# Two-layer hybrid block on one core: the feed-forward input is rated and split ahead, and two of three products become one of 512 columns

## The reference

```python
def rms_norm(x, g):
    y = xf * lax.rsqrt(jnp.mean(xf * xf, axis=-1, keepdims=True) + EPS)
    return y * g

def conv_ffn(h, w_up, conv_w, conv_b, w_down):
    u = h @ w_up                       # 256 x 1024 by 1024 x 5632
    u = conv_b + sum(conv_w[j] * causal_shift(u, 2 - j) for j in range(3))
    gate, val = jnp.split(u, 2, axis=-1)
    return (jax.nn.silu(gate) * val) @ w_down      # 2816 x 1024

x = x + conv_ffn(rms_norm(x, norm_ffn_g[l]), ...)
```

## Time and profile before

| | us |
|---|---|
| median of 3 runs | 1101.73 (1101.21 to 1103.01) |
| the profiled execution | 1100.96 |
| its span, first to last instruction | 1099.2 |
| PE busy | 1074.0 (98%) |
| weight loads busy (beside PE) | 1020.2 (93%) |
| DVE busy | 826.3 (75%) |
| ACT busy | 600.2 (55%) |

### The profile page before, as it was taken

The page is one execution under the profiler, slowest core; times in us unless marked ns, Lnnn a source line. Parts: engine busy times, 40 slices in busy tenths (PEclk is TensorE's granted clock), DMA queues, the critical chain, the costliest instruction groups (busy, mean ns, idle before and its releaser), DMA issues.

```text
span 1099.2 us, 26063 instructions
## 1 busy us (share of the span) xinstructions
PE 1074.0 (98%) x10078; PEld 1020.2 (93%) x10078; DVE 826.3 (75%) x1393; ACT 600.2 (55%) x891; POOL 10.5 (1%) x24
## 2 busy tenths in 40 slices
PE   8999999999999999999999999999999999999997
PEld 7998898898999999999999889988999999999996
DVE  6798485685787878887869975738767878888776
ACT  6951312666665655555678313137475666555555
POOL 0000000100000000000000000010000000000000
PEclk9999999999999999999999999999999999999998
DMA  8451322444355565555534413134445456555663
GB/s 292 150 173 60 115 79 78 122 138 147 123 174 172 170 194 185 179 173 189 191 119 154 154 59 113 45 106 133 137 147 177 142 170 194 186 175 174 190 185 105
DMA packets 46272, 164.00 MB, mean 149 GB/s; under 512 B 5904, under 2 KB 6080, under 8 KB 46192
## 3 DMA queue, kind: packets, MB, share of 16 engines
q1 hardware_dynamic: 44784, 160.88, 45.6%
q0 software_dynamic: 688, 0.81, 0.4%
q10 hardware_dynamic: 720, 1.14, 0.3%
HBM read 161.24 MB, written 1.05 MB: 148 GB/s over the span
## 4 chain that ended last, share of the span: by engine, by line
PE 88%; DVE 5%; ACT 4%; issue 2%; DMA 1%; SPq 0%; DVEq 0%; ACTq 0%
PE psum L429 87%; DVE sb_lo L1187 1%; ACT sb_rw L854 1%; DVE sb_rw L1265 1%; ACT sb_hi L854 1%; DVE sb_inv L1399 1%; ACT L854 1%; DMA sb_x<-x_t 1%; ACT sb_inv L854 0%; DVE sb_rw L1269 0%; ACT sb_oh L854 0%; DVE sb_rw L1505 0%; DVE sb_rw L1503 0%; ACT sb_rs L854 0%; DVE sb_ol L1206 0%
## 5 line engine op out<-in xcount | busy, mean ns | idle before, releaser
L854 ACT ACTIVATE sb_hi<-sb_raw 128x1024 fp32r<-128x1024 f32 (+1 forms) x300 | 312.0, 1049 | 262.9 <-PE psum L429 258.9
L429 PE MATMUL psum<-sb_hh,sb_hi 128*128 128x256 f32 x1568 | 450.6, 287 | 4.0 <-DVE sb_hl L1194 3.0
L429 PE MATMUL psum<-sb_hl,sb_hi 128*128 128x256 f32 x1568 | 443.6, 283 | 0.0
L429 PE MATMUL psum<-sb_hh,sb_lo 128*128 128x256 f32 x1568 | 443.4, 283 | 0.0
L1187 DVE TENSOR_TENSOR sb_lo<-sb_raw,sb_hi 128x1024 fp32r<-128x1024 f32 x298 | 361.0, 1221 | 72.5 <-ACT sb_hi L854 70.7
L429 PEld LDWEIGHTS psum<-sb_hh,sb_hi 128*128 128x128 f32 x1568 | 300.6, 192 | 10.7 <-issue 6.9
L429 PEld LDWEIGHTS psum<-sb_hl,sb_hi 128*128 128x128 f32 x1568 | 300.8, 192 | 1.0 <-issue 1.0
L429 PEld LDWEIGHTS psum<-sb_hh,sb_lo 128*128 128x128 f32 x1568 | 300.7, 192 | 0.0
L429 PE MATMUL psum<-sb_oh,sb_hi 128*128 128x256 f32 x672 | 193.1, 287 | 7.1 <-DVE sb_ol L1516 4.7
L429 PE MATMUL psum<-sb_oh,sb_lo 128*128 128x256 f32 x672 | 191.3, 285 | 0.0
L429 PE MATMUL psum<-sb_ol,sb_hi 128*128 128x256 f32 x672 | 191.2, 285 | 0.0
(11 more groups left out here) (165 smaller groups left out, 1002.3 us busy)
## 6 DMA issues: line engine op xcount, KB each, us to landing
sb_raw<-w_stream SPq DMA_DIRECT2D x299, 512.0 KB, 4.0
sb_pm<-mix_par ACTq DMA_DIRECT2D x2, 512.5 KB, 3.8
y_t<-sb_rw SPq DMA_DIRECT2D x4, 256.0 KB, 2.3
sb_cf<-const_f SPq DMA_DIRECT2D x1, 739.0 KB, 9.1
sb_pm<-mix_par SPq DMA_DIRECT2D x1, 512.5 KB, 9.7
sb_raw<-w_stream SPq DMA_DIRECT2D x2, 256.0 KB, 3.7
sb_x<-x_t SPq DMA_DIRECT2D x2, 256.0 KB, 4.8
sb_x<-x_t SPq DMA_DIRECT2D x1, 512.0 KB, 6.2
```

The costliest lines, as they stand in the source:

```text
L429: return pe.matmul(out, lhsT, rhs, start=start, stop=stop, skip_group_check=True)
L854: return act.activation(out, in_, func, scale=scale, bias=bias, **kw)
```

## The change

`hh` and `hl` (x times g) stay for tiles 0 to 5. During the first turn of the loop, which is written out now (tiles 2 to 5), DVE and ACT build a second input: x times g times the rates, in float32 (`XR`), its high half and its low half, which lie side by side in the new tensor `o2` (`RATED`, behind the places of `oh` and `ol`, which are now parts of `o2`). The 16 tiles of the four turns that follow multiply this input. The high weights meet high and low half in one matmul of 512 columns (high half's sum in columns 0 to 255 of the bank, low half's in 256 to 511), and the low weights meet the high half in a second matmul of 256. The two sums are joined on the way out: ACT copies columns 256 to 511 to `UM` (`low_half`), DVE adds columns 0 to 255 (`add_up`), which takes the place of `scale_up`. The rates are no longer multiplied there.

```diff
+        oh, ol = o2[:, 0, :, :], o2[:, 1, :, :]
+        RATED = o2[:, :, BT:, :]
+        XR = unit(4, 2).rearrange("p (k t) -> p k t", t=T)
@@ TensorE, ffn_up
+            out = bank[2 * (u % 2) + which]
             for k in range(KT):
+                if rated:
+                    mm(out, hi[:, s, cols], RATED[:, :, k, :], k == 0, False)
+                    last = mm(out[:, 0:T], lo[:, s, cols], RATED[:, 0, k, :], False, k == KT - 1)
+                else:
+                    last = split_mm(out[:, 0:T], ...)
@@ TensorE, the loop
-                with pe.Fori(0, FTURNS) as i:
+                turn(0, False)
+                pe.wait_ge(rated_l, 2 * l + 2)
+                with pe.Fori(1, FTURNS) as i:
+                    turn(i, True)
@@ ACT
+            def low_half(t, u, which, slab):
+                act.wait_ge(slab_done, slab + 1)
+                k = 2 * (u % 2) + which
+                do(UM[:, k, :], bank[k][:, T:2 * T], ACT.Copy).then_inc(low_out, 1)
@@ ACT, a tile of the loop (rated: turns 1 to 4)
                         for which in range(2):
+                            if rated:
+                                low_half(...)
                             conv(l, t, u, which, ..., True)
                         silu(l, t, u)
                         ahead_in(split, l, i, o + 2)
                         product(l, t, u)
+                        if not rated and u in (1, 2):
+                            four = slice(4 * u - 4, 4 * u)
+                            act.wait_ge(rated_x, 2 * l + u)
+                            do(RATED[:, 0, four, :], XR[:, four, :], ACT.Copy).then_inc(rated_h, 1)
@@ DVE
+            def add_up(l, t, u, which):
+                k = 2 * (u % 2) + which
+                dve.wait_ge(low_out, l * 2 * (FT - FU - 2) + 2 * t + (which + 1 - 2 * (FU + 2)))
+                tt(UM[:, k, :], UM[:, k, :], bank[k][:, 0:T], ALU.add).then_inc(up_scaled, 1)
+            def rate(l, u):
+                four = slice(4 * (u % 2), 4 * (u % 2) + 4)
+                if u < 2:
+                    for t in range(4 * u, 4 * u + 4):
+                        ins = stt(XR[:, t, :], x[:, t, :], pf[:, t:t + 1], rs[:, 0:T], ALU.mult, ALU.mult)
+                    ins.then_inc(rated_x, 1)
+                else:
+                    dve.wait_ge(rated_h, 2 * l + u - 1)
+                    tt(RATED[:, 1, four, :], XR[:, four, :], RATED[:, 0, four, :].bitcast(F32), ALU.subtract)\
+                        .then_inc(rated_l, 1)
@@ DVE, a tile of the loop
+                            if rated:
+                                add_up(l, t, u, which)
+                            else:
+                                scale_up(...)
...
                         product_lo(l, t, u)
+                        if not rated:
+                            rate(l, u)
```

More of the change, by code:

```diff
@@ L213, in hybrid_blocks @@
         hl = sb("hl", [P, KT, T], F32R)
-        oh = sb("oh", [P, 3 * BT, T], F32R)
-        ol = sb("ol", [P, 3 * BT, T], F32R)
+        o2 = sb("o2", [P, 2, 3 * BT, T], F32R)
         rw = sb("rw", [P, 11 * 1024 + 8])
@@ L312, in hybrid_blocks @@
         scaled = sem("scaled")
+        rated_x, rated_h, rated_l = sem("rated_x"), sem("rated_h"), sem("rated_l")
         zeros_set, zeros_used = sem("zeros_set"), sem("zeros_used")
@@ L327, in hybrid_blocks @@
         y_ready, y_stored = sem("y_ready"), sem("y_stored")
-        up_scaled = sem("up_scaled")
+        up_scaled, low_out = sem("up_scaled"), sem("low_out")
         tap2, conv_done = sem("tap2"), sem("conv_done")
@@ L333, in hybrid_blocks @@
                if k not in ("D", "E", "xs", "gsig", "prepa", "prepb", "rk", "kkn", "kkq", "lora", "gn3", "gn4", "rope")}
-        act_ = {k: sem("act_" + k) for k in TIMES if k not in ("D", "E", "xs", "norm")}
-        dve_ = {k: sem("dve_" + k) for k in TIMES if k not in ("D", "E", "xs", "norm")}
+        act_ = {k: sem("act_" + k) for k in TIMES
+                if k not in ("D", "E", "xs", "norm", "prepa", "prepb", "bon", "mat", "m1", "dxy", "rhs0", "s1", "rhs1",
+                             "rope", "gsig")}
+        dve_ = {k: sem("dve_" + k) for k in TIMES
+                if k not in ("D", "E", "xs", "norm", "lora", "up", "kkq", "natv", "natk", "u0", "u1", "o", "gsig",
+                             "ct", "cav")}
         dve_mid = {k: sem("dve_mid_" + k) for k in ("lam", "prepb", "bon", "cs", "crms")}
@@ L788, in step, with ffn_up @@
                     last.then_inc(pe_["crms"], 1)
-            def ffn_up(l, t, u, slab, s0_, first):
+            def ffn_up(l, t, u, slab, s0_, first, rated):
                 for which in range(2):
@@ L796, in ffn_up @@
                         pe.wait_ge(up_scaled, l * 2 * FT + 2 * t + (which - 3))
+                    out = bank[2 * (u % 2) + which]
                     for k in range(KT):
                         cols = slice(k * P, (k + 1) * P)
-                        last = split_mm(bank[2 * (u % 2) + which][:, 0:T], (hi[:, s, cols], lo[:, s, cols]),
-                                        (hh[:, k, :], hl[:, k, :]), k == 0, k == KT - 1)
+                        if rated:
+                            mm(out, hi[:, s, cols], RATED[:, :, k, :], k == 0, False)
+                            last = mm(out[:, 0:T], lo[:, s, cols], RATED[:, 0, k, :], False, k == KT - 1)
+                        else:
+                            last = split_mm(out[:, 0:T], (hi[:, s, cols], lo[:, s, cols]),
+                                            (hh[:, k, :], hl[:, k, :]), k == 0, k == KT - 1)
                     last.then_inc(slab_done, 1)
@@ L827, in _, with turn @@
                 norm(2 * l + 1)
-                ffn_up(l, 1, 1, at + 2, (FFN0 + 2) % RING, True)
+                ffn_up(l, 1, 1, at + 2, (FFN0 + 2) % RING, True, False)
                 ffn_down(l, 0, 0, at + 4, (FFN0 + 4) % RING, True)
-                with pe.Fori(0, FTURNS) as i:
+                def turn(i, rated):
                     for u in range(FU):
@@ L833, in _ @@
                         slab = l * SLABS + 3 * FU * i + (FFN0 + o)
-                        ffn_up(l, t, u, slab, (FFN0 + o) % RING, False)
+                        ffn_up(l, t, u, slab, (FFN0 + o) % RING, False, rated)
                         ffn_down(l, FU * i + (u + 1), u + 1, slab + 2, (FFN0 + o + 2) % RING, False)
+                turn(0, False)
+                pe.wait_ge(rated_l, 2 * l + 2)
+                with pe.Fori(1, FTURNS) as i:
+                    turn(i, True)
                 ffn_down(l, FT - 1, FT - 1, l * SLABS + SLABS - 1, (SLABS - 1) % RING, False, True)
@@ L1130, in _, with turn @@
                     product(l, t, t)
-                with act.Fori(0, FTURNS) as i:
+                def turn(i, rated):
                     for u in range(FU):
@@ L1137, in _ @@
                         for which in range(2):
+                            if rated:
+                                low_half(t, u, which, l * SLABS + 3 * FU * i + (o + which))
                             conv(l, t, u, which, 8 * FU * i + (8 + 8 * (u + 2) + 4 * which), True)
@@ L1141, in _ @@
                         product(l, t, u)
+                        if not rated and u in (1, 2):
+                            four = slice(4 * u - 4, 4 * u)
+                            act.wait_ge(rated_x, 2 * l + u)
+                            do(RATED[:, 0, four, :], XR[:, four, :], ACT.Copy).then_inc(rated_h, 1)
+                turn(0, False)
+                with act.Fori(1, FTURNS) as i:
+                    turn(i, True)
                 ahead(l, SLABS - 1)
@@ L1555, in _, with turn @@
                 before = own.n
-                with dve.Fori(0, FTURNS) as i:
+                def turn(i, rated):
                     own.base = l * DVE_OWN["layer"] + i * DVE_OWN["turn"]
@@ L1562, in _ @@
                             ahead_in(lambda m, s, used, landed: split(used + AHEAD, s, used, None), l, i, o + which)
-                            scale_up(l, t, u, which, l * SLABS + 3 * FU * i + (o + which))
+                            if rated:
+                                add_up(l, t, u, which)
+                            else:
+                                scale_up(l, t, u, which, l * SLABS + 3 * FU * i + (o + which))
                         for which in range(2):
@@ L1568, in _ @@
                         product_lo(l, t, u)
+                        if not rated:
+                            rate(l, u)
+                turn(0, False)
+                own.n = before
+                with dve.Fori(1, FTURNS) as i:
+                    turn(i, True)
                 assert own.n - before == DVE_OWN["turn"], ("dve turn", own.n - before)
```

## The result

The changed kernel takes 1109.4 us (median of 7 runs, 1105.1 to 1111.9), the kernel before 1101.2: slower by 0.71%, ratio 1.0071, 95% interval 1.0051 to 1.0090. The forecast was 1105.5 us, slower by 0.35%, with 1101.5 to 1109.5 as its range. The sign and the mechanism came out, the size is more than twice the forecast, and the median lies only 0.1 us inside the range. The profiled execution took 1110.16 us, with a span of 1108.4.

A forecast was written before the change was run, and what follows sets the result against it. The prediction took TensorE's own stream to bound the loop, with the DVE and ACT chain at its ends. Stream -6.7, pause +7.0, chain +0.9 and clock +2.6 gave +3.8 us, so 1105.5 us, range 1101.5 to 1109.5.

The forecast's parts named there:

- TensorE's stream: Rated tiles: 512 triples of 360 ns become pairs of 347 ns, each saving 13 ns, 6.7 us in all.
- The pause: Before up(6), TensorE waits for DVE's second low half of the rated input: 3.5 us per layer, 7.0 in all.
- DVE's lateness at the seam: Where up(6) starts, DVE's lateness adds up to 0.6 us to the pause; 0.4 was taken.
- The chain at down(21): At each layer's last block, the new ACT copy lengthens TensorE's wait by 0.42 us, 0.9 in all.
- The clock: Behind each new pause the clock falls to 1.2 GHz, costing 1.3 us per layer, 2.6 in all.
- The fixed part hidden in a pair (faster): Rival: a 512-column matmul beside one of 256 hides the weight load; 320 ns a pair, 1091.7 us; chance 0.13.
- The clock that stays up: Rival: the new pause costs no clock, or only in one layer; about 1103.1 us; chance 0.20.
- Much slower: Rival: two-piece operand makes pairs 356 ns, DVE's backlog makes pauses 4.5 us; +10.5 us, 1112; chance 0.09.
- The rival with the fixed part left in the pair: Removed matmuls save only 1.3 us, TensorE taking two pieces of 256 as two matmuls; 1110.9 us; chance 0.06.

The follow-up runs named there:

- experiment 6: The changed kernel with a slab's eight matmuls of 512 columns first and the eight of 256 behind them: 1105.67 us, ratio 1.0036 to the kernel before.
- experiment 4: The changed kernel with both low halves made behind tile 4 and the rated input multiplied in three matmuls of 256 columns: 1101.55 us, ratio 1.0012 to the kernel before.
- experiment 2: The changed kernel with the rated input built and waited for but not used, all tiles multiplied as before: 1109.16 us, ratio 1.0070 to the kernel before.
- experiment 1: The changed kernel with both low halves of the rated input made behind tile 4, the second one tile earlier: 1096.66 us, ratio 0.9960 to the kernel before.
- experiment 8: The changed kernel, tile 6 starting with the first low half and waiting for the second before its fifth weight row: 1102.11 us, ratio 1.0010 to the kernel before.
- experiment 3: The changed kernel with low halves made behind tile 4 and the rated input waited for but not used: 1100.71 us, ratio 0.9992 to the kernel before.
- experiment 5: The changed kernel with high and low half side by side in memory, so the 512 columns are one piece: 1108.60 us, ratio 1.0065 to the kernel before.

## Why the prediction was right in kind and short in size

**TensorE's stream: -6.7 forecast, -3.6 measured.** This is the term of the sum that was mis-sized, by 3.1 of the 4.4 us between forecast and result. I took the 512 columns at 227 ns from matmuls that stand among their like, and the 256 at 120 likewise. Alternating they make 353, so the saving is 512 x 7 ns and not 512 x 13. Of the 6 ns between 347 and 353, 3.4 come with the alternation (experiment 6). The rest is my reading of the rows: the mean among their like is 229 ns, not 227. The distance of 240, which is 236 before rounding, was a sign of it that I kept as a bound only. That the fixed part of a removed matmul is the gain was right (experiment 4). The Trainium skill (TensorE: Matmul & The Clock Gate, "Back-to-back issue gap") would have given 1.3 us by the 2.5 ns of its formula, which it gives for an isolated matmul. 7 ns were measured, about midway between that and my 13.

**The pause: +7.0 forecast, +6.8 measured.** It stands where it was said, at 3.23 us idle. The product's low half in tile 5 begins 1.59 us after down(4)'s last matmul (409.03 against 407.44), where it was 1.49 before (406.74 against 405.37 less one distance of 0.12), so that DVE's lateness at the seam was 0.1 us and not the 0.4 I took. The likely reason, not shown by a run of its own, is that the written-out turn has no register work between dependent instructions. The step from the product's low half to the next instruction took 0.34 and not 0.40. What I had as TensorE's own start, 0.15, was 0.36. These errors mostly cancel, and that the term came out so close is partly luck.

**The chain at down(21): +0.9 forecast, +0.84 measured** (2.19 against 1.77 us per layer; gone again in experiment 2).

**The clock: +2.6 forecast, 3.0 in the trace of the change, about 4 over the medians.** In the profiled execution half clock stands behind both pauses and costs some 1.5 us each (5 pairs at 640 instead of 353), as forecast. With it each layer's segment closes: -1.8 + 3.4 + 0.4 + 1.5 = +3.5, where +3.56 and +3.45 were measured. Over the runs the differences left after the pauses are larger or smaller: 5.9 us (change less experiment 1), 3.9 (less experiment 8), 1.7 (experiment 2 less experiment 3). I priced only the new pauses, and not that the clock also differs from kernel to kernel behind the waits that both have, at the layers' ends and in the attention part. So a kernel's medians carry a share of clock that no single place explains. Why it falls behind one wait and not behind another is not shown.

Without the clock the measured terms are -3.6 + 6.8 + 0.8 = +4.0. The difference between the medians is 8.2, so 4.2 are left. They are a remainder and not a measurement of their own. The mean granted clock supports them: 5 of the change's 7 runs had 0.988 or 0.989, among them the profiled one, whose trace has seven stretches of half clock with the one at its end. The trace of before, with 0.996, has three.

**The rivals.** The fixed part hidden in a pair (faster) is refuted by 353 ns. The clock that stays up happened in part, in single executions. "Much slower" named two causes: the two-piece operand is refuted (experiment 5), DVE's backlog was less than taken. The rival with the fixed part left in the pair, 1110.9 us, came nearer to the measured time than the forecast did, in part through the clock, which it took no higher than I did. About half of the 13 ns did stay in the pair, but its mechanism, two pieces of 256 taken as two matmuls, is refuted by experiment 5.

## What to carry to other kernels

A step that saves nanoseconds per instruction over hundreds of them can be lost at the one place where it is switched on: look for what the first use waits for, and finish that work one unit earlier, even if it crowds an engine that has slack. Here the same instructions, one tile earlier, turned 0.7% slower into 0.4% faster, of which the clock gave a part. Take the distance of two matmuls from the mean of many and not from one pair of rows, and from a stream that alternates like the new one. Price a pause of TensorE like the ones here (1.7 us or more) at its length plus some 1.5 us of clock, with a chance. And compare segments between fixed marks in two traces: they separated the terms to about 0.2 us, which the medians could not.

## What was not expected of the hardware

Whether the granted clock falls to 1.2 GHz behind an idle stretch is not settled by the stretch's length. Counted over the ten traces of this study, with the first 20 us left out, where short idle stretches follow each other closely: behind 1.52 us 0 of 2, behind 1.70 us 5 of 20, behind 1.77 us 6 of 6, behind 2.19 us 11 of 14, behind 3.2 us 5 of 8. Lengths within 0.04 us are counted together. In experiment 1 even the 2.19 us at the end of layer 0 left it up, where 1.77 brought it down in the kernel before:

```profile
544.00:547.30 3.30, 1.68 (x14) 1.71 (x15) 3.27 (x5) 2.65 (x3) 0.34 (x1) 1.00 0.37 99
547.30:550.70 3.40, 3.40 (x29) 3.31 (x29) 3.40 (x8) 3.24 (x8) 0.00 (x0) 1.00 0.71 243
```

Executions of one kernel differ the same way: of the 11 of experiment 4 those with a mean clock of 0.995 or more took 1100.6 to 1101.6 us, those with 0.992 took 1102.2 to 1104.3. Over the 29 runs of the kernel before on that chip, time and mean clock correlate at -0.85, so most of the spread goes with the clock. The attention part between the two feed-forward segments took 340.13 to 340.19 us in nine of the ten traces and 340.40 in that of experiment 3.
